# A two-layer streaming encoder in three-pass float32r: every low weight half subtracted on VectorE

## What is computed

```python
for l in range(DEPTH):                       # DEPTH = 2
    h = rmsnorm(x, norm1_g[l])
    proj = h @ w_in[l]                       # 2048 x 4352
    aq, ak, av, bq, bk, bv, cq, ck, cv = jnp.split(proj, splits, axis=-1)
    out_a = mixer_chunked_relbias(...)       # 8 heads, own chunk and 8 before
    out_b = mixer_swa_sinks(...)             # 16 heads, 128-frame window, sinks
    out_c = mixer_diff(...)                  # 4 heads, difference of two softmaxes
    x = x + jnp.concatenate([out_a, out_b, out_c], axis=-1) @ w_out[l]
    h2 = rmsnorm(x, norm2_g[l])
    x = x + jnp.square(jax.nn.relu(h2 @ w_up[l])) @ w_down[l]
```

## Time and profile before

| what | value |
| --- | --- |
| time, median of three runs | 2122.57 us (2121.98 to 2126.64) |
| the profiled execution's own time | 2122.87 us |
| its span, first to last instruction | 2121.0 us |
| TensorE busy | 2084.7 us of the span |
| VectorE busy | 1274.8 us |
| ScalarE busy | 1010.3 us |
| POOL busy | 197.6 us |
| mean granted TensorE clock | 0.999 of full speed |

### The profile page before, as it was taken

The page is one execution under the profiler, slowest core; times in us unless marked ns, Lnnn a source line. Parts: engine busy times, 40 slices in busy tenths (PEclk is TensorE's granted clock), DMA queues, the critical chain, the costliest instruction groups (busy, mean ns, idle before and its releaser), DMA issues.

```text
span 2121.0 us, 26490 instructions
## 1 busy us (share of the span) xinstructions
PE 2084.7 (98%) x10598; PEld 1738.0 (82%) x10598; DVE 1274.8 (60%) x1635; ACT 1010.3 (48%) x1353; POOL 197.6 (9%) x205
## 2 busy tenths in 40 slices
PE   7999999999999999999999999999999999999999
PEld 6877778888888888888878777788888888888887
DVE  6667556565565555556666675556655555565666
ACT  5456654443443444344445576544434434443444
POOL 2544120000000000000033431000000000000000
PEclk9999999999999999999999999999999999999999
DMA  8566786666666666666666568766666666666664
GB/s 262 163 183 169 178 230 178 189 189 195 190 189 191 191 189 195 190 189 190 185 175 181 159 177 204 202 182 187 194 192 189 190 196 190 189 190 194 189 192 149
DMA packets 209387, 400.70 MB, mean 189 GB/s; under 512 B 14862, under 2 KB 21872, under 8 KB 209264
## 3 DMA queue, kind: packets, MB, share of 16 engines
q1 hardware_dynamic: 203856, 381.85, 60.8%
q0 software_dynamic: 4608, 16.78, 4.3%
q10 hardware_dynamic: 800, 0.37, 0.1%
HBM read 380.05 MB, written 2.12 MB: 180 GB/s over the span
## 4 chain that ended last, share of the span: by engine, by line
PE 94%; DVE 2%; ACT 2%; issue 1%; DMA 1%; SPq 0%; DVEq 0%; POOL 0%; ACTq 0%; POOLq 0%
PE psum L475 22%; PE psum L439 19%; PE psum L441 19%; PE psum L440 18%; PE psum L478 12%; PE psum L485 1%; PE psum L545 1%; ACT w_hi L637 1%; DMA x<-in_x_dram 1%; PE psum L532 1%; PE psum L530 1%; DVE w_lo L806 1%; PE psum L571 0%; DVE probs L952 0%; DMA w_lo<-raw_ring 0%
## 5 line engine op out<-in xcount | busy, mean ns | idle before, releaser
L806 DVE TENSOR_TENSOR w_lo<-raw_ring,w_hi 128x1024 fp32r<-128x1024 f32 (+1 forms) x692 | 854.4, 1235 | 764.5 <-ACT w_hi L637 764.2
L637 ACT CAST w_hi<-raw_ring 128x1024 fp32r<-128x1024 f32 (+1 forms) x724 | 753.8, 1041 | 1006.5 <-PE psum L441 611.6
L475 PE MATMUL psum<-xt,w_hi 128*128 128x512 f32 x2048 | 512.9, 392 | 0.0
L439 PE MATMUL psum<-w_hi,ht_hi 128*128 128x512 f32 x1280 | 502.8, 393 | 1.3 <-DMA w_lo<-raw_ring 1.2
L441 PE MATMUL psum<-w_hi,ht_lo 128*128 128x512 f32 x1280 | 498.6, 390 | 0.0
L440 PE MATMUL psum<-w_lo,ht_hi 128*128 128x512 f32 x1280 | 498.3, 389 | 0.0
L475 PEld LDWEIGHTS psum<-xt,w_hi 128*128 128x128 f32 x2048 | 368.8, 189 | 66.3
L478 PEld LDWEIGHTS psum<-xt,w_lo 128*128 128x128 f32 x2048 | 279.4, 190 | 20.0
L478 PE MATMUL psum<-xt,w_lo 128*128 128x256 f32 x2048 | 285.6, 282 | 0.0
L439 PEld LDWEIGHTS psum<-w_hi,ht_hi 128*128 128x128 f32 x1280 | 240.3, 188 | 53.3 <-issue 5.1
L441 PEld LDWEIGHTS psum<-w_hi,ht_lo 128*128 128x128 f32 x1280 | 240.2, 188 | 50.8
(11 more groups left out here) (125 smaller groups left out, 1070.8 us busy)
## 6 DMA issues: line engine op xcount, KB each, us to landing
raw_ring<-in_w_up_dram SPq DMA_DIRECT2D x256, 512.0 KB, 3.7
raw_ring<-in_w_down_dram SPq DMA_DIRECT2D x256, 512.0 KB, 3.7
raw_ring<-in_w_in_dram SPq DMA_DIRECT2D x132, 512.0 KB, 4.2
raw_ring<-in_w_out_dram SPq DMA_DIRECT2D x64, 512.0 KB, 4.8
w_lo<-raw_ring POOLq DMA_DIRECT2D x32, 512.0 KB, 5.5
raw_ring<-in_w_in_dram SPq DMA_DIRECT2D x16, 256.0 KB, 2.8
x<-in_x_dram SPq DMA_DIRECT2D x4, 512.0 KB, 10.1
out_dram<-x SPq DMA_DIRECT2D x4, 512.0 KB, 3.9
```

The lines of the kernel that those rows point to most:

```text
L439: pe.matmul(out_ap, t_hi, m_hi, start=start, stop=False, skip_group_check=True)
L475: pe.matmul(bank[:, f, :], w_hi[:, w, j, f * P:(f + 1) * P], both, start=kt == 0, stop=False, skip_group_check=True)
L637: act.copy(w_hi[:, u % AHEAD, :, 0:cols], raw_ring[:, u % RAWS, :, 0:cols]).then_inc(hi_ready, 1)
L806: dve.tensor_tensor(w_lo[:, u % AHEAD, :, 0:cols], raw_ring[:, u % RAWS, :, 0:cols], w_hi[:, u % AHEAD, :, 0:cols].bitcast(F32), ALU.subtr ...
```

## The change

`SUMMED_UNITS` is gone. ScalarE no longer writes negated copies, POOL no longer issues the adding transfers, and VectorE's `split_lo` runs for every unit, at its place in the step. TensorE and SP wait on the one count `split_done` for every unit. POOL's two head norms follow each other without transfers between.

```diff
-SUMMED_UNITS = list(range(55, 87, 2))
-VECTOR_SPLITS = UNITS - len(SUMMED_UNITS)
-POOL_SCALES = {61: 6, 69: 7}
+POOL_SCALES = [6, 7]
...
             def load(pl, u, w, width, offset, cols):
-                if u - RAWS in SUMMED_UNITS:
-                    sp.wait_ge(*lo_sum_of(pl, u - RAWS))
-                else:
-                    sp.wait_ge(split_done, pl.at(VECTOR_SPLITS, vector_splits(u - RAWS + 1) + RAWS, LOOP_UNITS))
+                sp.wait_ge(split_done, pl.unit(u + 1))
...
             def unit_is_split(pl, u):
-                if u in SUMMED_UNITS:
-                    pe.wait_ge(*lo_sum_of(pl, u))
-                else:
-                    pe.wait_ge(split_done, pl.at(VECTOR_SPLITS, vector_splits(u + 1) + RAWS, LOOP_UNITS))
+                pe.wait_ge(split_done, pl.unit(u + 1 + RAWS))
...
                 act.copy(w_hi[:, u % AHEAD, :, 0:cols], raw_ring[:, u % RAWS, :, 0:cols]).then_inc(hi_ready, 1)
-                if u in SUMMED_UNITS:
-                    act.activation(w_lo[:, u % AHEAD, :, :], raw_ring[:, u % RAWS, :, :], ACT.Copy, scale=-1.0).then_inc(lo_negated, 1)
...
-                if u not in SUMMED_UNITS:
-                    split_lo(pl, u, PROJ[u // UPC][2] if u < PU else CW)
+                split_lo(pl, u, PROJ[u // UPC][2] if u < PU else CW)
...
-                for n, u in enumerate(SUMMED_UNITS):
-                    if u in POOL_SCALES:
-                        head_scale(l, POOL_SCALES[u])
-                    pool.wait_ge(lo_negated, pl.at(len(SUMMED_UNITS), n + 1))
-                    pool.dma_start(w_lo[:, u % AHEAD, :, :], raw_ring[:, u % RAWS, :, :],
-                                   accum_op=ALU.add).then_inc(lo_sum_of(pl, u)[0], 16)
+                for c in POOL_SCALES:
+                    head_scale(l, c)
```

More of the change, by code:

```diff
@@ L135, in lam_init @@
     return 0.8 - 0.6 * float(np.exp(-0.3 * layer))
-def vector_splits(n):
-    return n - sum(u < n for u in SUMMED_UNITS)
 def before(n, parity):
@@ L217, in encoder @@
         split_done = sem("split_done")
-        lo_negated = sem("lo_negated")
-        lo_summed = [sem(f"lo_summed{i}") for i in range(2)]
         unit_done = sem("unit_done")
@@ L280, in evictions @@
                 return self.at(EVICTIONS[p], before(chunk, p) + 1, LOOP_EVICTIONS)
-        def lo_sum_of(pl, u):
-            n = SUMMED_UNITS.index(u)
-            return lo_summed[n % 2], 16 * pl.at(len(SUMMED_UNITS) // 2, n // 2 + 1)
         def mlp_steps(first, kinds):
```

## The result

The changed kernel takes 2149.60 us (median of four runs, 2146.47 to 2152.64), the kernel before 2124.61 us beside it (2121.98 to 2127.33): a ratio of 1.0119, interval 1.0106 to 1.0132. That is 25 us slower. The prediction had +18.2 us on the 2122.87 us of the profiled execution, 2141 us, and a range of 2133.5 to 2149.5 us; the time lies 0.1 us above the upper end. The profiled execution took 2146.47 us, 23.6 more than that of before.

What follows compares the result with a forecast made beforehand. TensorE was taken to bound the kernel, so its new waits are not made up: 19.4 us over two layers, less 1.2 for removed transfers, +18.2 on 2122.87 gives 2141 us; range 2133.5 to 2149.5.

Steps and rivals of the forecast that it cites:

- The chain at an odd step: From odd hi copy start through subtraction, copy, masks, sums and scaling to TensorE's first transposition: 5.52 us.
- no loss: Rival: subtractions fit VectorE's idle time, leaving only the 1.2 us gain, 2121.7 us; chance 0.08, with shortened wait 0.03.
- the whole price: Rival: all 32 subtractions lie on the path at 1.23 us, +39.4 - 1.2, 2161 us; chance 0.03.
- The sum of the waits: TensorE's added waits for scaling, 9.7 us a layer, 19.4 in two, less 1.2 us for removed transfers: +18.2 us.
- the middle of the bounds: Pair 4's added wait taken as 1.5 us, between 0.26 (POOL done by the scaling) and 2.35 (subtraction stretched too).
- the longest waits at pairs 4 and 7: Expected sign in the changed profile: of TensorE's waits for VectorE's scaling, these two pairs' are longest.
- none, one or two falls: TensorE's clock drops behind pair 4's 3.1 us waits: 0 to 3 us; none in the forecast, two in the range.
- about 1.5 in all: Cost in us of one fall of TensorE's clock, of which 0.8 us in a 2 us window.
- my own list: Pair-by-pair added waits of TensorE in one layer, 9.7 us in sum, with 1.51 at pair 11.
- waits and clock together: Rival: dearer hand-overs, pair 4 at its upper end and two or more clock falls, 2150.6 us or more; chance 0.04.
- dearer hand-overs: Part of a rival: each of 24 pairs costs 0.2 us more than thought, 4.8 us.

Runs made afterwards that it cites:

- defer: Changed kernel with each layer's sixteen odd subtractions moved one step later, behind that step's scaling; 2125.12 us against 2125.93 for the kernel before, ratio 0.9995.
- tables_late: Changed kernel with POOL held back from the second layer's rotation tables until TensorE is past unit 90; 2149.69 us in one run.
- after_again: The changed kernel run once more, unaltered, for its clock record; 2148.28 us in one run.
- no_rope: Changed kernel without POOL's rotation of the last group B queries (chunk 5), so part of the computation is left out; 2139.99 us, ratio 1.0072.
- waits_only: Kernel before, adding transfers kept, with six multiplications by 1.0 ahead of the sums and scaling at pairs 4 and 11 of each layer; 2140.99 us, ratio 1.0067.
- behind_masks: Changed kernel with each odd subtraction at the end of its own step, behind copy, masks and panel; 2135.90 us, ratio 1.0040.
- defer2: Changed kernel with only units 55 and 69 subtracted one step later, relieving pairs 4 and 11; 2136.36 us, ratio 1.0042.
- best: Changed kernel with all odd subtractions one step later, pair 4 scaled at step 51, its first map copied earlier, POOL's tables late; 2122.57 us, ratio 0.9987.

## Why the prediction was right or wrong

**Direction and mechanism: right.** The chain at an odd step is the predicted one: 184.88 (hi copy) to 190.38 us is 5.50 us, where 5.52 was worked out. The rival "no loss" falls to the 25 us measured, and "the whole price" to the waits, +18.45 us and not 38.2; `defer`, with the same work and no loss, shows that the place in the queue decides.

**The sum of the waits: right.** TensorE's waits in the steps of the change were 2.46 and 3.62 us in the two layers before and 12.45 and 12.08 after: +18.45 us, predicted +18.2. Pair by pair, added us in one layer:

| pair | predicted | measured |
| --- | --- | --- |
| 4 | 1.5 (0.26 to 2.35) | 2.2 |
| 5, 8, 9 | 1.05 | 0.82 |
| 6 | 1.49 | 1.2 (1.39, less 0.20 that its second map waited before) |
| 7 | 1.18 | 1.05, and 0.42 at the values of step 58 |
| 10 | 0.78 | 0.66 |
| 11 | 1.51 | 2.17 and 1.75 |
| 12 | 1.2 | 0.89 |
| 13, 14 | 0.8 | 0.42 |
| 15 | 0.2 | 0.17 |

Smaller misses cancel, so that the sum came out within 0.3 us is in part luck. At pair 4 I took the middle of the bounds, hoping that POOL's work would be pushed back; it lay beside the scaling, 2.82 us instead of 2.25, and the upper end was near. At pair 11 POOL's tables were not foreseen (`tables_late`), nor was the panel of step 57, which now holds up a product of values by 0.42 us. I expected the longest waits at pairs 4 and 7; they came at pairs 4 and 11. The short pairs were 0.03 to 0.3 us cheaper than I said.

**The clock: the step that failed.** I wrote that pair 4's wait could bring "none, one or two falls", took none for the forecast, and kept two for the range. Five were profiled, against one in the kernel before, and in two further executions with nearly these waits 20.48 and 23.89 us at the lower level, as much as six and seven. The price of one was right, though the prediction doesn't show how its "about 1.5 in all" comes out of a 2 us stretch: 5/12 of the 3.41 us that a fall lasted is 1.42. Ten profiled executions give it too: the time, less TensorE's waits between 40 and 1400 us, less the time at which the first unit's first matrix product starts, against the us at the lower level (all in us):

| kernel | time | waits | at the lower level | start of first unit |
| --- | --- | --- | --- | --- |
| before | 2122.87 | 17.77 | 3.41 | 16.21 |
| changed | 2146.47 | 36.00 | 17.07 | 15.44 |
| `after_again` | 2148.28 | 36.15 | 20.48 | 15.70 |
| `tables_late` | 2149.69 | 36.39 | 23.89 | 15.12 |
| `no_rope` | 2140.66 | 31.18 | 13.65 | 15.30 |
| `waits_only` | 2139.65 | 29.28 | 17.07 | 16.64 |
| `behind_masks` | 2135.35 | 26.64 | 17.07 | 15.58 |
| `defer2` | 2134.13 | 29.97 | 0.00 | 16.40 |
| `defer` | 2125.12 | 19.36 | 6.83 | 15.75 |
| `best` | 2120.42 | 15.85 | 3.41 | 15.99 |

A line through them, 2087.4 us + 0.426 for each us at the lower level, meets all within 1.6 us; a stretch of 3.41 us costs 1.45, predicted "about 1.5". By it the profiled difference of 23.6 us is 18.2 of waits + 5.8 of clock (13.66 us more at the lower level) - 0.8 of an earlier start, which leaves 0.4. The changed kernel's other runs have no trace, but the slower ones tend to have the lower mean granted clock: 2146.47 us at 0.995, 2149.02 at 0.995, 2150.18 at 0.994, 2152.64 at 0.992. So the clock is most of what the median's +25 has over +18.2, shown in the profiled execution and only likely in the others.

So the number of falls was missed, by looking at one pair. Pair 11's wait had 1.5 us in my own list, and the earlier trace rows showed a fall behind a 2.34 us wait; both belonged to the count. In the ten traces every one of the 32 stretches stands at a wait of TensorE of 1.74 us or more: at all ten waits of 3.7 us and longer, and at 22 of the 64 between 1.7 and 3.0 us (counted from 20 us on). The rival "waits and clock together" named the right pair of causes, at 2150.6 us, but asked for dearer hand-overs as well, which were not there, and had 0.04.

**Open.** Which of the waits between 1.7 and 3.0 us brings a fall. Behind pair 11's 1.75 to 2.18 us it came in both layers of four executions (the changed kernel's two, `no_rope`, `tables_late`), behind 2.45 us of the same pair in `waits_only` in neither, behind the head norm's 2.34 us in some, behind pair 7's 1.74 us not in the changed kernel's two executions, but in the first layer of `tables_late`. In `defer`, `behind_masks` and `waits_only` one or two lie in the kernel's first 70 us, ahead of all that these kernels change. The runs give the price of a fall and that waits cause it, not the rule.

## What to carry to other kernels

A busy share of 60% says nothing on whether an in-order queue can take more work: ask which operation the new one stands ahead of, what it waits for itself, and whether the engine's idle time lies before or behind that point; one step later the same work cost 25 us less. Where TensorE is the bound, allow for a fall of the clock behind each new wait as long as those that brought one here (some from 1.74 us on, all from 3.7), and count such waits over all stages. Work taken off an engine lets its later work start earlier, beside something else: see beside what.

## What the runs showed of the hardware

- In an execution that keeps TensorE 97% busy, some single waits of 1.74 to 4.9 us, and all ten of 3.7 us and more, came with 3.41 or 6.83 us at a granted clock of 0.50, which began within 1.7 us of the wait's end, at some 1.45 us of time for 3.41; the number of such stretches is not a property of the program (five, six in two executions of one kernel).
- POOL's rotation beside VectorE stretched four scalings from 1.01 to 2.82 us and the sums from 0.16 to 0.73; small table work beside them stretched four scalings from 1.01 to 1.31.
